# Router logits in four column groups, joint selection rows, per-tile RMS norms and per-head learning-rate products

## Time and profile before

| | |
|---|---|
| runs | 3869.21, 3873.16, 3871.01 us; median 3871.01 |
| the profiled execution, its own time | 3877.7 us |
| its span | 3875.9 us, 71976 instructions |
| granted TensorE clock, mean | 0.923 of full speed |
| TensorE busy | 3258.5 us (84%) |
| DVE busy | 1533.0 us (40%) |
| ACT busy | 828.4 us (21%) |
| POOL busy | 273.1 us (7%) |

### The profile page before, as it was taken

One profiled execution on the slowest core, in us unless ns is written; L12 is line 12 of the kernel. 1 busy time (PEld: TensorE's weight loads), 2 busy tenths in 40 slices (PEclk: granted clock), 3 DMA queues, 4 the chain that ended last, 5 costly groups with the idle time before them and its releaser, 6 DMA issues. The chain is left out here.

```text
span 3875.9 us, 71976 instructions
## 1 busy us (share of the span) xinstructions
PE 3258.5 (84%) x31462; PEld 1890.5 (49%) x31462; DVE 1533.0 (40%) x3373; ACT 828.4 (21%) x1742; POOL 273.1 (7%) x254
## 2 busy tenths in 40 slices
PE   6997989979699897699999669978888837688787
PEld 5845568454344654334343234557777733322222
DVE  3655346562112752321222161157777762311111
ACT  2104211051111641000000100046655421000000
POOL 0000000010000200000000000001222210000000
PEclk9998899997899997799999889979999978799999
DMA  6663136601220112599999801000000012599998
GB/s 172 172 171 105 39 96 171 174 24 61 72 60 30 44 55 109 198 363 343 342 357 342 303 33 65 17 24 4 4 4 4 4 35 109 202 396 399 401 402 348
DMA packets 149196, 605.80 MB, mean 156 GB/s; under 512 B 19232, under 2 KB 22112, under 8 KB 131872
## 3 DMA queue, kind: packets, MB, share of 16 engines
q1 hardware_dynamic: 142560, 579.70, 41.6%
q0 software_dynamic: 6336, 21.63, 2.4%
HBM read 576.52 MB, written 31.07 MB: 157 GB/s over the span
## 5 line engine op out<-in xcount | busy, mean ns | idle before, releaser
L1704 PE MATMUL psum<-ring,big 128*64 128x512 f32 (+1 forms) x6144 | 909.8, 502 | 108.4 <-DMA ring<-moe_w 92.0
L1704 PEld LDWEIGHTS psum<-ring,big 128*64 128x64 f32 (+1 forms) x6144 | 302.7, 125 | 676.1 <-issue 474.7
L371 PE MATMUL psum<-h_uT,ring 128*128 128x264 f32 x1280 | 290.5, 387 | 0.0
L500 DVE SCALAR_TENSOR_TENSOR h_O<-h_O,cond_silu 128x512 f32<-128x512 f32 x336 | 226.8, 744 | 103.3 <-DMA h_O<-ada_w 103.2
L371 PEld LDWEIGHTS psum<-h_uT,ring 128*128 128x128 f32 x1280 | 242.0, 190 | 46.5 <-issue 5.8
L1215 PE MATMUL psum<-ring,big 128*128 128x512 f32 x576 | 249.4, 592 | 2.0 <-PEq L55 2.0
L2257 PE MATMUL psum<-ring,gates 64*64 64x128 f32 (+1 forms) x5120 | 172.6, 258 | 69.7 <-ACT ring L2438 64.5
L1850 DVE TENSOR_TENSOR big<-big,psum 128x512 f32<-128x512 f32 (+1 forms) x48 | 27.3, 596 | 465.4 <-PE psum L1704 465.4
L1985 PE MATMUL psum<-big,ring 128*128 128x512 f32 (+1 forms) x464 | 171.3, 532 | 31.7 <-DVE big L1956 24.0
L2257 PEld LDWEIGHTS psum<-ring,gates 64*64 64x64 f32 x5120 | 135.0, 135 | 85.5 <-DVE ring L2596 75.7
L1858 DVE SCALAR_TENSOR_TENSOR big<-psum,big,gates 64x512 f32<-64x512 f32 (+1 forms) x128 | 78.8, 615 | 244.9 <-PE psum L1704 243.5
(11 more groups left out here) (331 smaller groups left out, 4516.1 us busy)
## 6 DMA issues: line engine op xcount, KB each, us to landing
ring<-moe_w SPq DMA_DIRECT2D x192, 2048.0 KB, 10.6
h_O<-ada_w SPq DMA_DIRECT2D x192, 256.0 KB, 3.0
ring<-w_in SPq DMA_DIRECT2D x16, 2048.0 KB, 14.5
ring<-na_w_qkv SPq DMA_DIRECT2D x6, 2048.0 KB, 7.9
ring<-w_out SPq DMA_DIRECT2D x4, 2048.0 KB, 8.4
bias_rows<-na_table SPq DMA_DIRECT2D x16, 480.0 KB, 15.7
ring<-bias_rows SPq DMA_DIRECT2D x16, 360.0 KB, 3.0
rows<-big SPq DMA_DIRECT2D x10, 512.0 KB, 4.7
```

The source lines that it names most:

```text
L371: last = nc.tensor.matmul(bank(k, pair_bank(q) + h, NH), w[:, a, f * P:(f + 1) * P], uT[:, a, halves[h]], start=a == 0, stop=a == KD - 1)
L500: nc.vector.scalar_tensor_tensor(into, ada(u), by, into, ALU.mult, ALU.add).then_inc(s.acc, 1)
L1704: last = nc.tensor.matmul(bank(k, b, r.width)[q * r.n:(q + 1) * r.n, :], rowsT[:, half * HALF_K + n, r.first:r.first + r.n], w[:, n, q * r ...
```

## The change

1. `norm_turn` works tile by tile. DVE squares and sums tiles 0 and 1; ACT does the others, after a first square root on a constant. Each tile has its own square root (ACT), reciprocal and scaling (DVE), and TensorE transposes the blocks of a tile as soon as it is scaled; the banks of the first segment are full when its last tile is done. POOL's setting is gone.
2. `route` computes the logits with the tokens moving (512, then 256) and 32 router columns stationary (those of two feature blocks, of which 16 count), block `a` in column group `a % 4`. DVE and ACT copy the four partial sums to memory on chip, and a product with a matrix of ones and zeros (`pick`) adds them and puts the tokens back on the partitions. The affinities go to partitions 0 to 15 (512 tokens) and 32 to 47 (context) by products with the identity, in place of transposes, and are copied once, by stream. The first four rounds of the selection work on both; comparison, sum and the two operations after them are done once over 512 columns. Setting `ones` and `left` moves ahead of the logits.
3. In the scan `low_rank` computes the learning rates by head: sixteen products of 64 rows x 64 columns for the eight of 64 x 128, into the two halves of the output partitions.

```diff
 def turn_tensor(k, pe, s, src, segs, strided=False, normed=None):
...
     for tiles, rows, _ in segs:
-        for a in range(KD):
-            if j >= BANKS:
-                pe.wait_ge((s.act_turned, s.dve_turned)[j % 2], (j - BANKS) // 2 + 1)
-            for n, t in enumerate(tiles):
-                last = k.nc.tensor.transpose(bank(k, j % BANKS, rows, n * rows), ...
-            last.then_inc(s.turned, 1)
-            j += 1
+        for n, t in enumerate(tiles if j == 0 else []):
+            if normed is not None:
+                pe.wait_ge(normed, n + 1)
+            for a in range(KD):
+                last = k.nc.tensor.transpose(bank(k, a, rows, n * rows), ...
+                if n == len(tiles) - 1:
+                    last.then_inc(s.turned, 1)
+        done += len(tiles)
+        if j and normed is not None:
+            pe.wait_ge(normed, done)
+        for a in range(KD if j else 0):
+            pe.wait_ge((s.act_turned, s.dve_turned)[a % 2], (j + a - BANKS) // 2 + 1)
+            for n, t in enumerate(tiles):
+                last = k.nc.tensor.transpose(...)
+            last.then_inc(s.turned, 1)
+        j += KD
 def norm_turn(...):
         @block.scalar
-            act.wait_ge(s.cleared, 1)
-            for n, (t, rows) in enumerate(tiles):
-                nc.scalar.activation(junk[0:rows, :], src[0:rows, t, :], ACT.Square, accum_out=...)
-            act.wait_ge(s.summed, len(tiles))
-            nc.scalar.activation(stat[:, 1, :], stat[:, 0, :], ACT.Sqrt, bias=EPS, scale=1.0 / D)
+            def root(n): ...
+            nc.scalar.activation(stat[:, 1, 7:8], k.ones[:, 0:1], ACT.Sqrt)
+            act.wait_ge(s.first, 1)
+            root(0)
+            for n, (t, rows) in enumerate(tiles[2:], 2):
+                nc.scalar.activation(junk[0:rows, 0, :], src[0:rows, t, :], ACT.Square, accum_out=...)
+                if n == 2:
+                    act.wait_ge(s.first, 2)
+                    root(1)
+                act.wait_ge(s.summed, n - 1)
+                root(n)
         @block.vector
+            for n in range(2):
+                nc.vector.scalar_tensor_tensor(junk[0:rows, 1, :], src[0:rows, t, :], 1.0, src[0:rows, t, :], ALU.mult, ALU.mult,
+                                               accum_out=stat[0:rows, 0, n:n + 1]).then_inc(s.first, 1)
             for n, (t, rows) in enumerate(tiles):
+                dve.wait_ge(s.rooted, n + 1)
+                nc.vector.reciprocal(stat[0:rows, 2, n:n + 1], stat[0:rows, 1, n:n + 1])
+                dve.wait_ge(s.inverted, n + 1)
                 nc.vector.tensor_scalar(xn[0:rows, t, :], ...)
 def route(...):
         @block.tensor
-            for t in range(nt):
-                for a in range(KD):
-                    last = nc.tensor.matmul(bank(k, 0, EXPERTS, t * EXPERTS), hT[:, a, t * P:(t + 1) * P],
-                                            k.router[:, l, a, :], start=a == 0, stop=a == KD - 1)
+            for n, (_, first, width, _) in enumerate(streams):
+                for a in range(KD):
+                    q = a % 4
+                    last = nc.tensor.matmul(bank(k, n, width)[q * GROUP:(q + 1) * GROUP, :],
+                                            k.router[:, l, a // 2 * 2:a // 2 * 2 + 2, :]...,
+                                            hT[:, a, first:first + width], start=a < 4, stop=a >= 4)
+                last.then_inc(s.parts, 1)
+            pe.wait_ge(s.step, 3)
+            for n, (_, first, width, _) in enumerate(streams):
+                pe.wait_ge(s.copied, n + 1)
+                for t in range(first // P, (first + width) // P):
+                    last = nc.tensor.matmul(bank(k, 2, EXPERTS, t * EXPERTS), part[:, t * P:(t + 1) * P], pick[:, 0, :], ...)
...
-                last = nc.tensor.transpose(bank(k, 1, P, t * P)[0:EXPERTS, :], aff[:, t, 0:EXPERTS], k.ident[:, :])
+                last = nc.tensor.matmul(bank(k, 3 + (lo > 0), P, col)[lo:lo + EXPERTS, :], aff[:, t, 0:EXPERTS], k.ident[:, :], ...)
         @block.vector
-            for first, n, cap in streams:
-                row = left[:, first:first + n]
-                for _ in range(cap // 8):
-                    chain(nc.vector.max(best[:, :], row))
-                    chain(nc.vector.match_replace(row, best[:, :], row, -1.0))
+            for n in range(CAP_L // 8):
+                high = rows if n < CAP_C // 8 else EXPERTS
+                chain(nc.vector.max(best[0:high, :], left[0:high, :]))
+                chain(nc.vector.match_replace(left[0:high, :], best[0:high, :], left[0:high, :], -1.0))
 def low_rank(z, t, j, n):
                 for p in range(PAIRS):
-                    last = nc.tensor.matmul(bank(k, U(z) + 1, CH, p * CH), a2[lo:lo + CH, p * P:(p + 1) * P], ta[lo:lo + CH, at:at + CH], ...)
+                    for h in range(2):
+                        last = nc.tensor.matmul(bank(k, U(z) + 1, CH, p * CH)[h * CH:(h + 1) * CH, :],
+                                                a2[lo:lo + CH, p * P + h * CH:p * P + (h + 1) * CH], ta[lo:lo + CH, at:at + CH], ...)
```

More of the change, by code:

```diff
@@ L1514, in half_rows @@
     return slot.rearrange("p a b -> p (a b)").rearrange("p (a n) -> p a n", a=HALF_K)
+GROUP = 32
 def route(k, l, hT, xn, sums, aff, slot, tiles):
     nc = k.nc
[L1520 to L1521 removed]
+    streams = [(0, 0, SEQ, CAP_L)] + ([(GROUP, SEQ, CTX, CAP_C)] if len(tiles) > LT else [])
     nt = len(tiles)
[L1523 removed]
+    n_tok = nt * P
+    rows = streams[-1][0] + EXPERTS
+    with ExitStack() as mem, stage(k, "parts copied logits exped turned placed step ready") as (block, s):
         sb = lambda n, shape: mem.enter_context(nc.sbuf_tensor(f"{n}{k.stage_no}", shape, F32))
         stat = sb("stat", [P, 2, 8])
[L1526 to L1528 removed]
+        left, rank, ones = sb("left", [rows, SEQ]), sb("rank", [rows, SEQ]), sb("ones", [rows, SEQ])
+        part, pick = sb("part", [P, TOK2]), sb("pick", [P, 2, EXPERTS])
+        best = sb("best", [rows, 8])
         raw = sb("raw", [P, nt, EXPERTS])
+        at = lambda t: (0, t * P) if t < LT else (GROUP, (t - LT) * P)
         @block.sync
@@ L1557, in _ @@
         def _(act):
-            act.wait_ge(s.step, 4)
+            act.wait_ge(s.parts, len(streams))
+            for n, (_, first, width, _) in enumerate(streams[1:], 1):
+                act.wait_ge(s.copied, n)
+                nc.scalar.activation(part[:, first:first + width], bank(k, n, width), ACT.Copy).then_inc(s.copied, 1)
+            act.wait_ge(s.step, 9)
             nc.scalar.activation(raw[:, :, :], raw[:, :, :], ACT.Exp).then_inc(s.exped, 1)
@@ L1592, in _ @@
+            nc.vector.tensor_scalar(rank[:, :], rank[:, :], -1.0, None, ALU.add).then_inc(s.ready, 1)
             dve.wait_ge(s.placed, 1)
-            chain(nc.vector.tensor_copy(slot[:, 0:nt, 0:EXPERTS], bank(k, 3, nt * EXPERTS)
-                                        .rearrange("p (t e) -> p t e", t=nt)))
+            for n, (_, first, width, _) in enumerate(streams):
+                ts = slice(first // P, (first + width) // P)
+                chain(nc.vector.tensor_copy(slot[:, ts, 0:EXPERTS], bank(k, 5 + n, nt * EXPERTS)
+                                            .rearrange("p (t e) -> p t e", t=nt)[:, ts, :]))
```

74 lines of the change are left out of this document (42 added, 32 removed).

## The result

Changed kernel: **3785.24 us** (median of 4 runs, 3782.78 to 3788.00) against 3871.31 (4 runs), ratio 0.9775 [0.9763, 0.9788]: 86.1 us faster, where 66.5 were forecast. The two profiled executions, 3877.7 and 3784.0 us, differ by 93.7.

What follows compares the result with a forecast made beforehand. Norm and route stages were taken as chains ending in barriers, the scan as slots waiting for the learning-rate burst. Norms 30.5, routes 21 and scan 15 sum to 66.5 us: 3871.0 becomes 3804.5, range 3791 to 3826.

Steps and rivals of the forecast that it cites:

- rival 1: Scan gives nothing: records of one row half come no closer than 64 ns; 3819.5 us, chance 0.15.
- capped at 0.9 (1.8 at half clock): Scan: limit in us on the gain counted per slot from DVE's waits for the burst and the second level.
- for what is late next (ACT's N): Scan: reason for taking 15 us in place of 17; the second level also needs ACT's N.
- its 17: Scan: gain in us from adding both DVE waits over the slots that wait, capped per slot.
- in slots where DVE has more to do it waits for neither, and these give nothing: nine of 24: Scan: nine slots were to gain nothing, as DVE there waits for neither the burst nor the second level.
- the 0.7 net that affinities and copies were to cost: First route: affinities' products lose 1.1 us, one copy less saves 0.4.
- The four rounds (3.8): First route: four selection rounds over 256 columns go, saving 3.8 us.
- 3 more: Routes: extra gain in us if the products ran at full clock.
- the pace behind the first tile: Norms: TensorE sets the pace at 1.63 us per tile; in the second mixture the first bank is full at 9.1.
- rival 2: Norms copy- and DVE-bound earlier, from dearer DVE squares or TensorE stalls: 18 us rather than 30; 3817 us, chance 0.12.
- Rival 3: Scan: loads of one row half wait for each other and for matmuls, 48 us lost; 3867.5 us, chance 0.03.
- Rival 4: Slower: scan loses its full clock, with all 24 slots cold 3996 us; chance 0.02.

Runs made afterwards that it cites:

- idle transposes: Changed kernel plus sixteen identity transposes before TensorE's wait in each norm stage: 3796.26 us; also with early exponential table, 3799.90; with that and 16 constant products, 3788.95.
- the routes stand alone: Kernel before with only the two route stages changed: 3843.78 us, ratio 0.9925.
- the norms alone: Kernel before with only the six norm stages changed: 3840.73 us, ratio 0.9921.
- the rates alone: Kernel before with only the scan's learning rates computed head by head: 3847.97 us, ratio 0.9936.
- the orders: Changed kernel with the burst running all first heads, then all second, and the route's logits taking each column group's two rounds in a row: 3794.83 us, ratio 0.9795.
- the 32 products: Changed kernel plus 32 small products of constants on TensorE in the very first stage, where it is idle: 3805.50 us, ratio 0.9824.

## Why the prediction was wrong

The mechanisms were right in the main. What failed are the sizes of three terms of the sum, all too small, and a term that the sum put at nothing. One profile of before and one of after can't show this, since each has its own spells below full clock; the same stage averaged over all profiled kernels that have the same code in it can (us, from first to last instruction):

| | forecast | measured | old form, new form |
|---|---|---|---|
| six norm stages | 30.5 | 35.9 | 113.6 (three kernels), 77.7 (eight) |
| two routes | 21 | 24.2 | 77.2 (three), 53.0 (eight) |
| scan | 15 | 20.2 | 584.8 (three, without before), 564.6 (six, without those with idle transposes) |
| two experts' stages, same code | 0 | 5.1 | 1169.0 (three), 1163.9 (nine) |

That makes 85.4 of the 86.1 us. The other stages together take 1869.3 us before and 1869.2 in the changed kernel, and between 1866 and 1878 in the others, so that each row is good to one or two us.

- **Part 3, 15 us forecast, 20.2 measured with the last slot.** The burst is as forecast (1.0 us taken, 1.10 found, and 0.91 for 32 more), so rival 1 fell with its 64 ns. The step that failed is the price of a slot: "capped at 0.9 (1.8 at half clock)", and the two us taken off "for what is late next (ACT's N)". The first ten slots, in each of which DVE waited, gave 13.7 where the cap allows 11.7: 2.1 each at half clock, where the burst is 1.75 shorter, and 1.06 each behind. Why a slot gains more than its burst is open. The two us for ACT's N did not show. In the fourteen later slots the 6.5 measured (20.2 less 13.7) are near the 5.4 that the forecast's rule gives there, by luck: its 17 took in four late waits of before, of which two (2.29 and 1.96 us) are the half-clock spells that the other kernels don't have. These wait in three late slots each, for 1.3 to 2.6 us together. So "in slots where DVE has more to do it waits for neither, and these give nothing: nine of 24" had no fixed nine to stand on: the slots without a wait are others in each execution.
- **Part 2, 21 forecast, 24.2 measured** (17.9 + 5.4 in the changed kernel, 20.3 + 6.8 where the routes stand alone). First route: softmax 12.8 us earlier where 10.9 were forecast (4.48 for the products forecast at 5.0; the adding products at 126 ns a record, not 200, since they ran at a granted clock of 1.00), and the 0.7 net that affinities and copies were to cost did not show: 3.2 us from the affinities' end to the first maximum in both. The four rounds (3.8) and the last steps (1.2, less 0.2) are as forecast. At full clock the products take 2.79 us, 1.7 less, and 1.92 in the second, 1.4 less: the forecast's "3 more". In the second route the forecast overlooked ACT's table load, exposed once the products are short, 1.28 us.
- **Part 1, 30.5 forecast, 35.9 measured by the stages.** The median of the norms alone, 29.7, seems to confirm the sum, but its interval reaches from 22 to 38; the stages of that kernel are 36.3 us shorter. The largest shortfalls are hybrid 1 (3.1 forecast, 4.6 measured), neighbourhood attention (4.2, 5.6), first mixture (6.8, 8.0) and RWKV (7.2, 8.1). The step that failed is the pace behind the first tile. TensorE started after 3.4 us (forecast 4). With 1.63 us per tile the first bank was to be full at 9.1 and copied from 9.3; in RWKV 32 transposes take 5.79 us (forecast 6.54) and the first copy starts at 8.5, as the clock rises within the stage:

```profile
2184.00:2186.00 2.00, 2.00 (x12) 2.00 (x11) 1.93 (x5) 1.05 (x3) 0.00 (x0) 0.50 0.00 0
2186.00:2188.00 2.00, 1.80 (x16) 1.60 (x15) 1.07 (x3) 1.08 (x2) 0.00 (x0) 0.96 0.00 0
```

  And DVE's four full and four half copies behind it take 4.77 us, for 4 x 0.81 + 4 x 0.54 = 5.4. The stage takes 13.4 us (forecast 14.9), the second mixture 12.2 (12.7). In the second mixture the transposes' early start is worth nothing.
- **What the forecast put at nothing.** The two experts' stages are 3.2 and 1.9 us shorter in the kernels with the new routes, with the same code in them. They come right behind the routes; no run took them apart, and the cause stays open. That such a stage can move by 20 us with the count of instructions ahead of it was shown, but both before and after have three stalls (11.7 and 12.3 us), so this is not it.
- **What looks like giving back.** Hybrid 0's forget logits run at half clock in the changed kernel, 6.64 us for 3.73. That is not shown to come from the norms: with the rates alone, whose norms are the old ones, they take 5.42, and with the orders, whose norms are the new ones, 3.73.
- **The range.** Its low end, 3791, had taken 19 for the scan and 38 for the norms, but nothing for the experts' stages. The rivals: rival 2 didn't happen (norms 36, not 18). Rival 3 neither: the Trainium skill (TensorE: Matmul & The Clock Gate, Part 3, The mechanism) lets a load overlap running matmuls only where the row group differs. Here all 32 loads use one row half and the records still start 29 ns apart, so the rule doesn't hold in that form; with the same columns each time, 1.84 us, it comes nearer. Rival 4 neither: the scan's clock behind the first three slots was 1.00 with the new burst.

## What to carry to other kernels

Price a change at a shared engine by doubling the cost first: which slots wait for an instruction differs from execution to execution, so the waits of one profile say too little. Before comparing two profiles, take the same stage from a third kernel whose code there is unchanged; the one execution of before held 6 us of slow spells, and the sum over the stages found 5 us in the norms that the median of the norms alone hid. And when a stage with unchanged code gets longer, count TensorE's stalls "for nothing" at a loop's jumps, and look for instruction packets in them, before explaining it.

## What the runs showed of the hardware

The hardware loop of the first experts' stage stalls TensorE at each jump back, once or twice, for 3.4 to 4.9 us each time, until a packet of 16,384 bytes of instructions has come. By where the loop's first instructions stand it is once or twice: with 128 instructions added ahead of the loop (64 weight loads and 64 products or transposes; with the 32 products the page has 72,767 for 72,639) the waits of the three jumps were 23.5 to 24.9 us in three kernels, with 192 added 12.2, and in the eleven other profiled kernels 11.7 to 13.0. The Trainium skill (Runtime: NRT & Kernel Launch, Terms) has an engine's instructions refilled in blocks of 16 KiB, and by its file listing (What's in a NEFF) an instruction has 64 B; that would make 256 instructions a block. The traces agree with both: packets of 16,384 bytes, and one more for each 256 TensorE records added. The 128 that bring the second stall are then half a block. That the loop's start then stands two records ahead of a block's end is inferred from the two records between the stalls; no row shows its place.

Products in four column groups overlap as well when the group changes with every second product as when it changes with each, where their records are long: 3.35 us for 16 records of 512 columns in both orders. Short records (64 columns) in two column halves need the change: 1.10 us for 32 when it alternates, 1.84 when it changes once.
